# Mixers of a two-block transformer kernel: the turn of values goes behind the value products, and the scaling of the first mixer's outputs becomes a step of its own

## The reference, cut to what matters

```python
qa, ka, va = jnp.split(pa, 3, axis=-1)          # 4 heads; per head 2 maps, 64 wide, values 128 wide
s = jnp.einsum("bqhmd,bkhmd->bhmqk", qb, k) * scale + t5_bias(...)
p = jax.nn.softmax(s, axis=-1)
a = p[:, :, 0] - lam * p[:, :, 1]
o = jnp.einsum("bhqk,bkhe->bqhe", a, v)
o = rms_norm(o, subln_g) * (1.0 - lam_init)      # per token and head, over 128 values
...
merged = (jax.nn.sigmoid(xn @ w_gate[0]) * (ya @ w_branch[0])    # branch 1 (A2)
          + jax.nn.sigmoid(xn @ w_gate[1]) * (yb @ w_branch[1])  # branch 2 (B2), grid neighbourhood
          + jax.nn.sigmoid(xn @ w_gate[2]) * (yc @ w_branch[2])) # branch 3 (C2), window of 128
return merged @ w_out
```

## Time and profile before

| what | value |
|---|---|
| median of 3 runs | 2272.96 us (2269.9 to 2273.39) |
| profiled execution, its own time | 2269.36 us |
| span of the profiled execution | 2267.6 us |
| mean granted TensorE clock | 0.996 |
| phase `mixers` on PE | about 1253.5 to 1840 us |

### The profile page before, as it was taken

The page is one execution under the profiler, slowest core; times in us unless marked ns, Lnnn a source line. Parts: engine busy times, 40 slices in busy tenths (PEclk is TensorE's granted clock), DMA queues, the critical chain, the costliest instruction groups (busy, mean ns, idle before and its releaser), DMA issues.

```text
span 2267.6 us, 35995 instructions
## 1 busy us (share of the span) xinstructions
PE 2207.2 (97%) x12576; PEld 1816.6 (80%) x12576; DVE 1239.6 (55%) x2661; ACT 904.0 (40%) x1815; POOL 220.9 (10%) x201
## 2 busy tenths in 40 slices
PE   8999999999999999999999899999999999999998
PEld 6577766778888889999999787777777787888887
DVE  6778776567737745443442555444555655433442
ACT  5566444444424443322232344444444443322332
POOL 0100143310000030000001000111100130000001
PEclk9999999999999999999999999999999999999999
DMA  4112112235533432342333222333433233332332
GB/s 122 34 41 56 52 43 57 84 114 148 155 98 95 121 115 84 93 125 86 92 97 103 62 81 81 86 96 94 99 95 95 81 98 93 93 108 79 99 102 75
DMA packets 400393, 205.93 MB, mean 91 GB/s; under 512 B 66908, under 2 KB 393928, under 8 KB 400284
## 3 DMA queue, kind: packets, MB, share of 16 engines
q1 hardware_dynamic: 399365, 204.09, 31.5%
q10 hardware_dynamic: 919, 0.43, 0.1%
HBM read 202.21 MB, written 14.80 MB: 96 GB/s over the span
## 4 chain that ended last, share of the span: by engine, by line
PE 82%; DVE 4%; ACT 2%; issue 2%; POOL 0%; DVEq 0%; ACTq 0%; POOLq 0%
PE acc L1171 53%; PE acc L1477 16%; PE acc L1221 5%; PE sco L1512 2%; PE acc L1576 1%; DVE w_lo L2276 1%; PE acc L1572 1%; PE sco L1265 1%; PE sco L1552 1%; PE acc L1312 1%; PE acc L1552 0%; PE sco L1532 0%; PE acc L1299 0%; DVE bias L2264 0%; PE sco L1289 0%
## 5 line engine op out<-in xcount | busy, mean ns | idle before, releaser
L1713 ACT ACTIVATE w_hi<-raw 128x512 fp32r<-128x512 f32 (+4 forms) x656 | 372.0, 614 | 693.3 <-PE acc L1171 659.4
L2276 DVE TENSOR_TENSOR w_lo<-raw,w_hi 128x512 fp32r<-128x512 f32 (+4 forms) x656 | 422.9, 685 | 141.6 <-ACT w_hi L1713 137.1
L1171 PE MATMUL acc<-xn_hi,w_hi 128*128 128x512 f32 (+1 forms) x1408 | 421.0, 340 | 2.1 <-DVE qbuf L2835 2.1
L1171 PE MATMUL acc<-xn_lo,w_hi 128*128 128x512 f32 (+1 forms) x1408 | 422.0, 340 | 0.0
L1171 PE MATMUL acc<-xn_hi,w_lo 128*128 128x512 f32 (+1 forms) x1408 | 420.9, 340 | 0.0
L1171 PEld LDWEIGHTS acc<-xn_hi,w_hi 128*128 128x128 f32 x1408 | 242.3, 188 | 35.6 <-DVE qbuf L2835 3.0
L1171 PEld LDWEIGHTS acc<-xn_lo,w_hi 128*128 128x128 f32 x1408 | 241.1, 188 | 30.9 <-issue 0.5
L1171 PEld LDWEIGHTS acc<-xn_hi,w_lo 128*128 128x128 f32 x1408 | 241.9, 189 | 29.8
L1171 PE MATMUL acc<-hid_lo,w_hi 128*128 128x512 f32 (+1 forms) x832 | 261.8, 349 | 0.0
L1171 PE MATMUL acc<-hid_hi,w_lo 128*128 128x512 f32 (+1 forms) x832 | 260.6, 348 | 0.0
L1171 PE MATMUL acc<-hid_hi,w_hi 128*128 128x512 f32 (+1 forms) x832 | 259.8, 347 | 0.8 <-DVE hid_lo L2777 0.8
(11 more groups left out here) (399 smaller groups left out, 3046.7 us busy)
## 6 DMA issues: line engine op xcount, KB each, us to landing
raw<-in_w_ffn_in SPq DMA_DIRECT2D x176, 256.0 KB, 3.0
raw<-in_w_in SPq DMA_DIRECT2D x118, 256.0 KB, 3.1
raw<-in_w_up SPq DMA_DIRECT2D x88, 256.0 KB, 3.0
raw<-in_w_ffn_out SPq DMA_DIRECT2D x32, 384.0 KB, 3.3
raw<-in_w_gate SPq DMA_DIRECT2D x48, 256.0 KB, 3.0
raw<-in_w_ffn_out SPq DMA_DIRECT2D x32, 320.0 KB, 3.7
raw<-in_w_out SPq DMA_DIRECT2D x32, 256.0 KB, 3.0
bias<-grids_dram SPq DMA_DIRECT2D x64, 128.0 KB, 3.0
```

The lines of the kernel that those rows point to most:

```text
L1171: mm = pe.matmul(acc[0:m, 2 * slot + b, 0:size], w[slot][:, t, 0:m], x[:, place(t), c:c + size], start=(t == 0 and w is w_hi and x is xh), ...
L1713: act.activation(w_hi[slot][:, a:b, :], raw[slot][:, a:b, :], ACT.Copy).then_inc(S[f"hi_ready{slot}"], parts)
L2276: dve.tensor_tensor(w_lo[slot][:, a:b, :], raw[slot][:, a:b, :], w_hi[slot][:, a:b, :].bitcast(F32), ALU.subtract).then_inc(S[f"split{slot ...
```

## The change

Two moves. First, in `work_of_mixers`, the entry "vturn" stands behind the value or both entry that followed it, in all nine places inside the loop (vturn 1 to 8 and 10). The pieces of projection between the entries stay at their positions in the list, so between pair and value there is now what stood between pair and vturn. Second, the reciprocal and the four multiplications leave `take_low` and become `scale_outputs`, which DVE issues at value 4, 8 and 12 and at both 16, ahead of `take_output` or `take_both`. No instruction is added or removed.

```diff
@@ work_of_mixers, events_of, first branch
+                yield ("value", v)
+                yield None
                 if v == mine[-1]:
                     yield from values_turned()
-                yield ("value", v)
-                yield None
                 if v == mine[0]:
                     yield from outputs_turned()
@@ the other branches
+            yield ("both", p)
+            yield None
             if v == mine[-2]:
                 yield from values_turned()
-            yield ("both", p)
-            yield None
             if v == mine[0]:
                 yield from outputs_turned()
@@ VectorE, mixers
-                def take_low(turn):
-
-                    name, i = TURNS[turn]
-                    hi, lo = (x[:, i, META:T] for x in outputs[name])
-                    x, g = TURNED["oturn", turn], GAIN["subln_gain_2"]
+                def scale_outputs(turn):
+
+                    i = TURNS[turn][1]
                     dve.wait_ge(S["o_root"], n.at("o_root", i + 1))
                     dve.reciprocal(o_rstd, o_root).then_inc(S["o_rstd"], 1)
                     dve.wait_ge(S["o_rstd"], n.at("o_rstd", i + 1))
...
                     last.then_inc(S["o_scaled"], 1)
+
+                def take_low(turn):
+
+                    name, i = TURNS[turn]
+                    hi, lo = (x[:, i, META:T] for x in outputs[name])
+                    x, g = TURNED["oturn", turn], GAIN["subln_gain_2"]
                     dve.wait_ge(S["pt_a"], n.at("pt_a", x + 1))
...
                     elif what == "value":
+                        if j % 4 == 0 and j > 0:
+                            scale_outputs(j // 4 - 1)
                         take_output(j)
...
                     elif what == "both":
+                        if j == 16:
+                            scale_outputs(3)
                         take_both(j)
```

## The result

The changed kernel takes 2254.15 us (median of 4 runs, 2251.69 to 2257.7), against 2273.18 us (2269.9 to 2274.5) for the kernel before, run beside it. The ratio that the runs give is 0.9922, 95% interval [0.9907, 0.9937]: 17.7 us less (14.3 to 21.1); the two medians alone differ by 19.0 us. The profiled execution took 2253.97 us with a span of 2252.2, 15.4 us less than before.

A forecast was written before the change was run, and what follows sets the result against it. TensorE was taken to bound the mixers, busy 554.27 of 586.50 us. Gains of 7.05 + 1.64 + 4.34 = 13.0 us, taken from the 2272.96 us median, gave 2260.0 us, range 2254 to 2268.5.

The forecast's parts named there:

- the forecast case: Whole kernel: TensorE's waits in the mixers go as reckoned, 10 to 16 us won; chance 0.63.
- rival (a): Mixers: only some of the gain comes, scaling late or turns waiting for meta values; 8.7 or 6.0 us won; chance 0.23.
- (b): Mixers: gain given back as TensorE meets waits for weights, scores or mixed maps; 2270 to 2275 us; chance 0.09.
- about 19: Sign in the profile after: TensorE's idle in the mixers falls from 32 to about 19 us, else the prediction is wrong.
- the sum: Whole kernel: the gains 7.05, 1.64 and 4.34 us added, 13.0 us won.
- Part 1: Turn of values: TensorE's waits for VectorE's scoring of the pair issued just before go, 7.05 us won.
- Part 2: Projection behind the copy of k: ScalarE's root comes sooner, two waits of 1.07 us fall to 0.25; 1.64 us won.
- Part 3: Turn of outputs: 5.45 us of waits behind VectorE's scaling shrink, 0.37 left at three for the copy of q; 4.34 won.
- The spares: Copy of meta values ready 1.1 us before turn 9 needs it; scaling ready 0.5 us before the turn of outputs.
- The table switch: ScalarE's table load taken as 1.28 us without the skill page's 1380 ns drain; with it, gain near 9 instead of 13.

The follow-up runs named there:

- the scaling alone: Kernel before the change with only VectorE's output scaling moved to values 4, 8, 12 and both 16, the list as before: ratio 0.9975 to the kernel before.
- only the first branch: Changed kernel with the turns of values of the second and third branch back at their old places: ratio 0.9948 to the kernel before.
- the turn ahead of the pair: Changed kernel, but the turn of values goes ahead of the pair it followed, value and root left at their old places: ratio 0.9979 to the kernel before.
- two added switches: Changed kernel with a tiny exponential and a tiny root added behind each of the four roots on ScalarE: ratio 0.9977 to the kernel before.
- one more switch: Changed kernel with one tiny exponential added behind each of the four roots on ScalarE: ratio 0.9926 to the kernel before.

## Why the prediction was right

**Direction and mechanism.** The mechanism of the forecast case came, not that of rival (a) or (b): TensorE's idle in the mixers fell from 32.4 to 18.5 us, where "about 19" was to be seen.

**The time** was forecast less well than the waits. The predicted 2260.0 us was 5.8 us too long, and the 2254.15 measured lie only 0.15 us inside the lower end of the range. The gain of 17.7 us (14.3 to 21.1) is above the 10 to 16 of the forecast case and its interval leaves out the 13.0 of the sum; only the profiled execution, 15.4 us faster, lies between 10 and 16. That the median fell inside the range is partly luck. Of the 5.8 us, 2.4 lie between the profiled execution (2253.97) and its forecast (2256.3); the term mis-sized below is most of it. The other 3.4 come from the 3.6 us by which the median before stood above its profiled execution. I carried this difference, and after the change it is 0.2 us. Such differences are the spread between executions, and it goes with the granted clock: of 21 later runs of the kernel before on one chip, those at 0.998 took 2266.3 to 2268.2 us and those at 0.994 or 0.995 took 2271.4 to 2274.6.

**Part 1** was priced at 7.05 us. All seven waits are gone, and they come back one by one where the list is put back (the scaling alone, only the first branch). That the turn waited for the scoring, and not for the tanh that the profile names, shows at turn of values 8 in the trace before, where ScalarE had long been idle:

```profile
1669.84 0.63 DVE L2610 CUSTOM_DVE_ANT_0 aux<-sco,bias,small 128x400 f32<-128x400 f32 x1
...
1671.08 0.39 ACT L2018 ACTIVATE v_tok<-acc 128x256 f32<-128x256 f32 x1 [4.73 <-PE acc L1591]
```

The scoring ended at 1670.47 and TensorE went on at 1670.59. With the turn ahead of the pair none of these waits is there either.

**Part 2** was priced at 1.64 us and measured 2.15: the waits for the copy of k were 0.43, 1.07, 1.07 and 0.32 us, and are 0.25, 0.24, 0.25 and 0. The two large ones went as reckoned. The two small ones that I left out gave the other 0.5; before the change they were

```profile
1338.81 0.47 PE L1477 MATMUL acc<-xn_hi,w_hi 128*128 128x512 f32 x1 [0.43 <-ACT kbuf L1964]
...
1475.68 0.47 PE L1477 MATMUL acc<-xn_hi,w_hi 128*128 128x512 f32 x1 [0.32 <-ACT kbuf L1964]
```

**Part 3** was priced at 4.34 us. 5.45 us became three waits of 0.34 for the copy of q, as forecast with 0.37: 4.43 us.

**The spares.** From the end of the value products I reckoned the copy of the meta values done at 5.4 us and turn 9 there at 6.5. Measured from the same point (1374.52) it is 5.3 and 6.2, a spare of 0.9 instead of 1.1; the turn of values took 0.46 us from start to start and not 0.71. The scaling had 0.35 us to spare and not 0.5. Both were enough, and neither by much. I took the spare at value 7 for that of all four heads, and read only TensorE, VectorE and ScalarE for it. At the third head it is 0.26 us, where VectorE's split took longer beside GpSimd's mask. That this still sufficed was luck: the sum did not look at GpSimd.

**The term mis-sized** is the worth of a wait. The three parts' idle fell by 7.05 + 2.15 + 4.43 = 13.6 us and all idle by 13.8 (a wait of 0.23 us for `w_lo` went too), but the stretch by 15.8. An idle time counts from the modelled end of the last matmul, and the next could have begun sooner: the matmuls of a projection are shown 0.39 us long and start every 0.23. Where a wait goes entirely, some 0.15 us more than its idle comes back. I had named this as a bound of part 1 and priced it at nothing; for the ten places without idle now it gives 1.5 us, and 13.8 + 1.5 = 15.3. The other kernels bear the size out, though none was built for it. In the column "rest" of the table, 38 and 37 idles go with 552.9 us, 33 with 551.5 to 552.0, and 27 to 29 with 550.7 to 551.3, so some 0.2 us for each, and 13.8 + 10 x 0.2 is the 15.8 measured. With only the first branch changed, five waits of 4.9 us together cost 5.5.

**The table switch.** Rows and runs put a switch at the load of 1.28 us alone: the tiny functions begin 0.01 us behind it, and an added switch costs 1.5 us with its function. The Trainium skill (ScalarE: Activation LUTs, What ACT_TABLE_LOAD costs) adds a drain of about 1380 ns to each. No run here shows it. With it the waits at the turn would have stood in the changed kernel already, whose spare is 0.9 us; the measurement decides.

**Where I was wrong** was in my own alternative, the turn ahead of the pair: I followed the moved entry's own instructions and forgot those that other code hangs on it.

## What to carry to other kernels

When one engine sets the end and a list sets everybody's order, look for the entry that waits for work issued just before it, and put other ready work between the two. Before moving it, count what rides along (here the split of weights and the root's place against the copies of k) and compute the spare of each thing that is late next; spares of 0.9 and 0.3 us held, and one more table switch would have used them up. Compute the spare at each repetition of the place, and with every engine that works beside it, since the smallest was three times smaller than the one looked at. Do not add a wait's idle alone: expect somewhat more than it where the wait goes entirely.

## What the runs showed of the hardware that was not expected

After some idles of about 2 us TensorE's granted clock fell to its lower level. The windows of 2 us of the turn ahead of the pair, behind the idle of 2.11 us (columns as in the earlier trace rows; the clock is third from the end):

```profile
1384.00:1386.00 2.00, 0.38 (x4) 0.14 (x2) 0.64 (x2) 1.99 (x5) 0.00 (x0) 1.00 0.01 4
1386.00:1388.00 2.00, 1.52 (x5) 1.20 (x6) 0.84 (x3) 1.98 (x3) 0.00 (x0) 0.73 0.10 29
1388.00:1390.00 2.00, 2.00 (x8) 1.24 (x8) 0.00 (x0) 1.99 (x6) 0.00 (x0) 0.50 0.80 237
1390.00:1392.00 2.00, 2.00 (x11) 1.43 (x8) 1.76 (x4) 0.72 (x2) 0.00 (x0) 0.91 0.00 0
```

0.50 is 1.2 of 2.4 GHz, and the matmuls start every 0.43 us instead of 0.23. The lost clock is (0.27 + 0.50 + 0.09) x 2 = 1.7 us, nearly as much as the idle itself.

The idle of 1.95 us near 1289, which every kernel here has, was followed by such a stretch in 6 of 12 profiled executions. The first profiles before and after the change are both among the six, so their comparison is not touched. With two added switches one of three idles of 2.06 was followed by it and the one of 3.22 was not. In the mixers' stretch no idle of 1.77 us or less was. What decides it in a given execution is open. So one profile does not tell what the clock costs a kernel on average: each new idle of this length is also a new chance to lose 1.7 us, as in the turn ahead of the pair.

VectorE's subtraction can slow down beside GpSimd's mask addition. Between 1400 and 1500 us of the changed kernel and the one with one more switch, every piece `w_lo` of 128 x 512 that has no mask addition beside it takes 0.68 or 0.69 us. The pieces that took longer, 0.88 to 1.62 us, all began while an addition was running, and all ended 0.5 to 0.6 us after it ended, as if they had waited it out. Pieces that were already running when an addition began were not slowed. That is a pattern of two traces; no run moves the mask addition by itself, so the cause is not shown.
